# An expert stage's first weight slots: which engine makes their low parts, and when block ends are compared

## The reference

```python
p_group = softmax(xf @ wr_g + br_g)               # 4 groups
p_top, g_sel = top_k(p_group, 1)
fine = (xf @ wr_e + br_e) of the chosen group     # 8 experts of it
e_val, e_sel = top_k(fine, 2)
# each token goes to 2 of 32 experts; an expert's tokens are laid out in blocks of 128 rows
y_rows = (silu(x_rows @ w_gate[e]) * (x_rows @ w_up[e])) @ w_down[e]     # per block
out[token] += y_rows * gate
```

## Time and profile before

| | us |
|---|---|
| median of three runs | 3236.76 |
| lowest and highest | 3235.91, 3239.71 |
| the profiled execution, from first to last instruction | 3237.1 |
| busy in it: TensorE, VectorE, ScalarE, GpSimd | 2982.9, 2440.3, 1418.8, 411.4 |

### The profile page before, as it was taken

How to read it: one execution, slowest core, us unless ns; L and a number is a source line. 1 busy time by engine, 2 the same in 40 slices (tenths; PEclk the granted TensorE clock), 3 DMA queues, 4 the chain that set the end, 5 groups by cost and what they waited for, 6 DMA issues and landing times. The chain is left out here.

```text
span 3237.1 us, 40575 instructions
## 1 busy us (share of the span) xinstructions
PE 2982.9 (92%) x13996; PEld 2406.9 (74%) x13996; DVE 2440.3 (75%) x2653; ACT 1418.8 (44%) x1698; POOL 411.4 (13%) x233
## 2 busy tenths in 40 slices
PE   7998999999989999889979999995989979999995
PEld 6777788877777878666767888884765767888884
DVE  4566888565567995576968999996487668999996
ACT  1233211022323110272336777774336327777775
POOL 0110112301101113100000000001323100000001
PEclk9998999999989999989979999997998979999997
DMA  4241765232325663164229999994213249999994
GB/s 168 66 163 66 235 208 169 104 128 86 144 92 164 215 199 113 53 191 111 84 105 368 382 372 369 388 370 160 91 40 126 94 163 385 380 374 391 385 387 157
DMA packets 346505, 667.23 MB, mean 206 GB/s; under 512 B 21936, under 2 KB 138604, under 8 KB 338172
## 3 DMA queue, kind: packets, MB, share of 16 engines
q1 hardware_dynamic: 339612, 642.58, 56.2%
q0 software_dynamic: 6752, 22.81, 2.1%
HBM read 612.20 MB, written 53.13 MB: 206 GB/s over the span
## 5 line engine op out<-in xcount | busy, mean ns | idle before, releaser
L2810 DVE TENSOR_TENSOR expert_w_low<-expert_w_raw,expert_w_high 128x2048 fp32r<-128x2048 f32 x290 | 663.4, 2289 | 65.4 <-ACT expert_w_high L2771 65.2
L2771 ACT CAST expert_w_high<-expert_w_raw 128x2048 fp32r<-128x2048 f32 x290 | 555.1, 1915 | 191.7 <-PE bank L144 180.8
L142 PE MATMUL bank<-expert_w_high,expert_x_high 128*128 128x512 f32 x928 | 379.5, 409 | 6.7 <-DVE expert_w_low L2810 4.5
L142 PE MATMUL bank<-first_XH,first_w_high 128*128 128x512 f32 (+1 forms) x944 | 369.9, 392 | 0.0
L144 PE MATMUL bank<-expert_w_high,expert_x_low 128*128 128x512 f32 x928 | 365.3, 394 | 0.0
L143 PE MATMUL bank<-expert_w_low,expert_x_high 128*128 128x512 f32 x928 | 363.9, 392 | 0.0
L143 PE MATMUL bank<-first_XL,first_w_high 128*128 128x512 f32 (+1 forms) x944 | 363.1, 385 | 0.0
L144 PE MATMUL bank<-first_XH,first_w_low 128*128 128x512 f32 (+1 forms) x944 | 362.8, 384 | 0.0
L222 DVE TENSOR_TENSOR first_w_low<-first_w_raw,first_w_high 128x2048 fp32r<-128x2048 f32 (+2 forms) x94 | 287.1, 3054 | 3.2
L220 DVE CAST first_w_high<-first_w_raw 128x2048 fp32r<-128x2048 f32 (+2 forms) x94 | 111.6, 1188 | 173.2 <-PE bank L144 152.1
L1440 ACT ACTIVATE ffn_conv<-bank,ffn_taps 128x512 f32<-128x512 f32 x88 | 68.4, 780 | 358.4 <-PE bank L144 358.4
(11 more groups left out here) (521 smaller groups left out, 5970.6 us busy)
## 6 DMA issues: line engine op xcount, KB each, us to landing
expert_w_raw<-in_moe_w_gate_dram SPq DMA_DIRECT2D x116, 1024.0 KB, 8.3
expert_w_raw<-in_moe_w_up_dram SPq DMA_DIRECT2D x116, 1024.0 KB, 13.0
expert_w_raw<-in_moe_w_down_dram SPq DMA_DIRECT2D x58, 1024.0 KB, 14.0
modulation<-in_moe_w_down_dram SPq DMA_DIRECT2D x58, 1024.0 KB, 14.0
ffn_mod_w<-in_ada_w_dram SPq DMA_DIRECT2D x48, 1024.0 KB, 4.9
first_w_raw<-in_w_up_dram SPq DMA_DIRECT2D x88, 512.0 KB, 6.6
first_w_raw<-in_w_down_dram SPq DMA_DIRECT2D x22, 1024.0 KB, 4.8
first_w_raw<-in_w_in_dram SPq DMA_DIRECT2D x20, 1024.0 KB, 5.0
```

The source lines that it names most:

```text
L142: nc.tensor.matmul(out, rounded(st[0]), rounded(mv[0]), start=start, stop=False)
L2771: nc.scalar.copy(rounded(high[:, part_of(e, n), :]), weights.place(place)).then_inc(w_high, 1)
L2810: nc.vector.tensor_tensor(rounded(low[:, part_of(e, n), :]), weights.place(place), high[:, part_of(e, n), :], ALU.subtract).then_inc(w_spl ...
```

## The change

Slots are named one to three for the first three of the first block (numbers 0 to 2 in the code). Slot one's low part goes from VectorE, ahead of the wait for the counts, to GpSimd, ahead of its wait for the token numbers. Slot two's low part stays on VectorE ahead of the wait for the lists and now also waits until slot one's has been counted. Slot three's low part goes from VectorE, behind the rows of the first block, to GpSimd, behind the second gather and ahead of its wait for the table. The comparison L2377 moves from ahead of the lists to behind the token numbers and the marks of used rows. In the first step of the loop VectorE's low parts wait for the count of those before them.

```diff
-    def on_vector(self, dve, before_rank, before_list):
+    def on_vector(self, dve, before_list):
...
-        before_rank()
         dve.wait_ge(self.ranked, 1)
...
-        link(V.tensor_tensor(all3(self.ends_at), self.block_end[:, :].rearrange("p (o e) -> p o e", o=1).to_broadcast([P, BLOCKS, E]),
-                             c2["index_block"].rearrange("p (s o) -> p s o", o=1).to_broadcast([P, BLOCKS, E]), ALU.is_le))
         before_list()
         dve.wait_ge(self.listed, 1)
         listed = self.LIST[:, 0:BLOCKS]
         link(V.tensor_scalar(self.token[:, :], listed, 1.0, 0.0, ALU.subtract, ALU.max))
         V.tensor_copy(G["slot_token"][:, :], self.token[:, :]).then_inc(self.slots_ready, 1)
         V.tensor_scalar(self.valid[:, :], listed, 0.5, None, ALU.is_gt).then_inc(self.marked, 1)
+        link(V.tensor_tensor(all3(self.ends_at), self.block_end[:, :].rearrange("p (o e) -> p o e", o=1).to_broadcast([P, BLOCKS, E]),
+                             c2["index_block"].rearrange("p (s o) -> p s o", o=1).to_broadcast([P, BLOCKS, E]), ALU.is_le))
         link(V.tensor_reduce(self.block_exp[:, :], all3(self.ends_at), AX_X, ALU.add))
...
+            def first_low(n):
+                number, place, _ = slot(Step(0), n)
+                pool.wait_ge(w_high, number + 1)
+                if n:
+                    pool.wait_ge(w_split, number)
+                nc.gpsimd.tensor_tensor(rounded(low[:, part_of(Step(0), n), :]), weights.place(place), high[:, part_of(Step(0), n), :], ALU.subtract
+                                        ).then_inc(w_split, 1)
+
+            first_low(0)
             pool.wait_ge(chain.slots_ready, 1)
             gather(0)
             gather(1)
+            first_low(2)
             pool.wait_ge(chain.table_set, 1)
...
                 dve.wait_ge(w_high, number + 1)
+                if e.j is None and e.odd == 0:
+                    dve.wait_ge(w_split, number)
...
-            chain.on_vector(dve, lambda: weight(Step(0), 0), lambda: weight(Step(0), 1))
+            chain.on_vector(dve, lambda: weight(Step(0), 1))
             for half in range(2):
                 rows(None, half)
-            for n in range(2, PARTS):
-                weight(Step(0), n)
             chain.gates_on_vector(dve)
```

## The result

| | before | after |
|---|---|---|
| median of seven runs, us | 3235.51 | 3244.89 |
| lowest and highest | 3230.61, 3239.71 | 3239.38, 3250.45 |
| span of the profiled execution | 3237.1 | 3237.5 |
| ratio to before | | 1.0029, interval [1.0020, 1.0038] |

The change makes the kernel slower by 9.4 us (interval 6.5 to 12.3). The forecast was 3241.8 in a range to 3244.6, 5.0 us above a median before of 3236.76: the sign was right, the size too small, and the time lies 0.3 us outside. With all seven runs that median is 3235.51, so the time alone hides 1.3 us of the miss.

What follows compares the result with a forecast made beforehand. It took each expert stage's head, from router's choice to first product, as the bound; 2 x (2.43 + 0.05) = 5.0 us gave 3241.8 us in the runs' terms, with an 8-in-10 range of 3237.6 to 3244.6.

Steps and rivals of the forecast that it cites:

- step g: GpSimd's gathers beside the moved comparison: up to 0.3 us more on a gather, taken as 0.
- Step a: Slot one on GpSimd: its subtraction holds VectorE's chain at L2357 until 1689.33, making the chain 1.6 us later.
- rival 2: Only two-SBUF-input or long VectorE operations are held; +1.6 us a stage, 3240.0 us; 20%.
- Step b: Slot two behind the lists' masks, comparison moved away: lists end at 1697.92, token numbers start 1.12 us later.
- Step c: Slot three on GpSimd: its subtraction holds L2386, so the block table is ready 6.7 us later.
- Step d: TensorE waits for the table, so each stage's first product comes 2.4 us later.
- Steps e: Loads of the second block, issued at 1707.9 instead of 1701.24, still land in time: cost 0.
- step f: VectorE's new wait in the first block delays slots seven and eight: 0.05 us a stage.
- 1: Rival: nothing on VectorE is held, first product 1.4 us earlier a stage, 3234.0 us; 4%.
- 3: Rival: the gathers' rows wait for GpSimd's slot three subtraction, delaying transposes and first product; 3245.2 us; 12%.
- 4: Rival: the second block's loads become late after all, 3246 us; 2%.

Runs made afterwards that it cites:

- cmp_back: The changed kernel with the comparison put back ahead of the wait for the lists; profiled once, heads 24.59 and 24.32 us (25.56 and 25.53 in the changed kernel).
- after_pad: The changed kernel plus 32 one-column GpSimd memsets in an early phase, which shift GpSimd's later code; 3239.49 us, ratio to before 1.0016.

## Why the prediction was wrong

The mechanism of the holds was right, and most of the cost lies where it was said. The step that failed is g, the price of a gather beside the comparison; the head of the second stage was taken too long in before, and the list of places had nothing behind the stages.

*Step a held.* The scan ended at 6.58 us; the forecast's end of the hold was 1689.33, 6.45 us. The held operation was not L2357 but the scan behind it, since the 128x1 operation passes. That is rival 2's reading of this place, and it made the token numbers +0.80 instead of +1.12 us.

*Step b held as far as the token numbers.* Slot two's low part fitted into the wait for the lists, and TensorE, not VectorE, released the token numbers.

*Step g failed*: "Up to 0.3 us on a gather [...]; I take 0." It was 1.1 us in each stage, outside my own bound, and cmp_back shows 1.0 and 1.2 us of head for it. The bound came from the loop's gathers. Fifty of these in before, those that take 1.12 to 1.25 us, start about 0.4 us before the end of a two-input subtraction of 2.29 us (L2810) and end 0.74 to 0.82 us behind it; the four that take 0.87 to 0.91 us have no such subtraction beside them. So the rows showed the same wait, but only its last 0.4 us. The trace of before had rows with more of it, in the phase behind the stage:

```profile
2226.08 1.28 DVE L2881 SCALAR_TENSOR_TENSOR attn_room<-attn_room,gate 128x1024 f32<-128x1024 f32 x1 [1.25 <-DMA attn_room<-y_rows,y_row]
2226.84 1.34 POOL L2870 DMA_INDIRECT attn_room<-y_rows,y_row  x1 [6.39 <-DMA attn_room<-y_rows,y_row]
...
2228.12 1.22 DVE L2888 TENSOR_TENSOR x_tokens<-x_tokens,attn_room 128x1024 f32<-128x1024 f32 x1
2228.48 1.68 POOL L2870 DMA_INDIRECT attn_room<-y_rows,y_row  x1 [0.30 <-issue]
```

Both gathers end 0.82 us behind VectorE's operation (2227.36 and 2228.18, 2229.34 and 2230.16). By these rows the gather beside the comparison would have been priced at 1.48 - 0.26 + 0.82 = 2.0 us (it starts 0.26 behind the comparison), not 0.94.

The Trainium skill, in SBUF — State Buffer, section "SBUF: two separate sides", states both sides of this: an operation of VectorE with two SBUF inputs takes the shared port pair only against a GpSimd operation that reads SBUF, and a box there warns that a DMA issued by GpSimd waits for VectorE, as GpSimd writes the descriptors itself. I had used its first half for VectorE's waits and not turned it round. The runs agree with the first (the scan 0.22 us under the writing, 2.56 under the subtraction). The box names fast one-input operations; here it was a two-input one that held the gather, and a 128x1280 reduction beside the same gather did not (1.11 us).

*Step c held* in its mechanism. The second subtraction started at 18.96 instead of 18.22 us (step g), took 4.51 instead of 4.60, and the table was ready at 24.55 instead of 24.11.

*Step d held*: first product 1.01 us behind the table. In stage one the head was 0.43 us longer than forecast. In stage two it was 1.08 longer, because I took its head of before for the same as stage one's. There the rows land earlier, so the transposes start at 19.41 us against 20.09 and the head is 0.68 shorter in before; a head set by the table gets none of that back. By the spread of landings above, part of these 0.68 us is chance of the one trace of before.

*Steps e and f*: SyncE's second loads came at 1701.77, 25.54 us (25.0 forecast), and the stage's first to last product took 505.45 us against 506.91. No load was late (ScalarE waited for no load in the first 60 us of either stage), and no cost of the new wait can be seen.

*What lies outside the heads.* The heads were forecast at 4.9 us together and measured at 6.4; step f's 0.1 us is in neither. Nothing in the prediction looked behind the stage. There the stretch to differential attention is 2.0 us longer in the trace: 0.3 us are left of GpSimd's late gather, and about 1.7 come from a stretch of low clock whose cause these runs do not settle. Without step g's 2.2 us of head, or without the low stretch, the time would by these numbers have come out inside the range; that it lies just outside is thus partly chance. How the 9.4 us of the medians divide beyond the 6.4 of the heads stays open.

*The rivals.* 1 (nothing held) is refuted. 2 is half right: the chain passed the 128x1 operation and was held at the scan, but at the table a CAST and a TENSOR_SCALAR of 128x40, which it let pass, were held for 5.04 and 5.17 us. 3 came near in time (3245.2) and is false: the transposes started at 21.79 us, while GpSimd was subtracting. 4 is refuted: no load was late.

## What to carry to other kernels

A port held for a whole instruction must be priced in both directions: who on VectorE waits for GpSimd, and which of GpSimd's gathers waits for VectorE. Splitting work between the two engines gained nothing here, with such operations in the chain next to it; putting the work behind the chain was worth 3.4 us of heads here, with no new engine in it. And a delay must be followed to where it counts: GpSimd's first gather of a later phase came 2.4 us late because its code lay elsewhere, 0.3 us of that were left 130 us on (0.7 against after_pad), and the larger part of the difference was TensorE's clock. Where a change is worth a few us, compare the granted clock of the two traces stretch by stretch before explaining the difference by the edit's logic.

## What was not expected of the hardware

- A hold can begin ahead of GpSimd's record: behind a gather, operations of VectorE issued 0.40 to 0.67 us before it were held (128x1 ones apart), those issued 0.69 us or more before passed. No run has such an operation just ahead of a subtraction without a gather before it.
- GpSimd writing only (5.22 us) holds a 128x40 one-input TENSOR_SCALAR (2.97 us) and lets two-input operations and reductions pass.
- Where GpSimd's code lies moves its first gather of the next phase by 2.1 to 2.4 us, of which 0.3 us against before and 0.7 against after_pad were left 130 us on.
- Behind the same pause of TensorE, 2.71 us, the granted clock fell to 0.50 for 3.4 us in eight of thirteen traces and stayed at 1.00 in five.
